# A ring of 24 weight slots, not 20, with rows gathered per expert from the residual stream

## The reference

```
def ec_moe(h, router_w, w_gu, w_down):
    cap = EC_CAPACITY_FACTOR * n // N_EXPERTS          # 32 rows for each expert
    aff = jax.nn.softmax(einsum('bnd,de->bne', h, router_w), axis=-1)
    gates, idx = lax.top_k(jnp.swapaxes(aff, 1, 2), cap)
    xs = jax.vmap(lambda hb, ib: hb[ib])(h, idx)
    ...
        gu = jnp.einsum('bcd,df->bcf', xe, wgu)        # 1024 x 4096 for each expert
        ga, up = jnp.split(gu, 2, axis=-1)
        return jnp.einsum('bcf,fd->bcd', jax.nn.silu(ga) * up, wd)   # 2048 x 1024
    ...  # times the gates, added back to the rows they came from

x = x + ec_moe(rmsnorm_2(x, norm_ffn_g), router_w, expert_w_gu, expert_w_down)
return rmsnorm_2(x, final_norm_g)
```

## Time and profile before

| | |
|---|---|
| median of 3 runs | 1543.46 us (1542.45 to 1544.28) |
| span of the profiled execution | 1539.7 us, from its first to its last instruction; no other time of that execution is given |
| PE, DVE, ACT, POOL busy | 77%, 29%, 25%, 6% of the span |
| moved by DMA | 504.89 MB, of it 493.98 MB on SP's queue |

### The profile page before, as it was taken

One profiled execution on the slowest core, in us unless ns is written; L12 is line 12 of the kernel. 1 busy time (PEld: TensorE's weight loads), 2 busy tenths in 40 slices (PEclk: granted clock), 3 DMA queues, 4 the chain that ended last, 5 costly groups with the idle time before them and its releaser, 6 DMA issues.

```text
span 1539.7 us, 19403 instructions
## 1 busy us (share of the span) xinstructions
PE 1192.7 (77%) x8282; PEld 697.3 (45%) x8282; DVE 443.8 (29%) x867; ACT 381.3 (25%) x847; POOL 87.8 (6%) x95
## 2 busy tenths in 40 slices
PE   7999999999997997986666676666666666666765
PEld 6898989999976775330221211211211212212112
DVE  4565776545678764110000000000000000000002
ACT  4655556444565653110000000000000000000002
POOL 0000010000134420000000000000000000000001
PEclk9999999999999998997877867868767768778666
DMA  8335455454653478999999999999999999999996
GB/s 316 138 137 219 166 189 222 174 195 165 209 191 110 137 273 324 414 421 421 422 421 422 421 422 421 421 421 421 421 422 421 421 422 421 421 421 421 421 421 275
DMA packets 72645, 504.89 MB, mean 328 GB/s; under 512 B 8944, under 2 KB 9584, under 8 KB 12400
## 3 DMA queue, kind: packets, MB, share of 16 engines
q1 hardware_dynamic: 68544, 493.98, 79.3%
q10 hardware_dynamic: 4016, 9.69, 1.8%
HBM read 502.58 MB, written 1.05 MB: 327 GB/s over the span
## 4 chain that ended last, share of the span: by engine, by line
DMA 51%; PE 35%; DVE 5%; ACT 3%; issue 3%; POOL 1%; SPq 1%; ACTq 0%; DVEq 0%; POOLq 0%
DMA RING<-in_wgu_dram 48%; PE PB L99 33%; DMA RING<-in_wdn_dram 2%; PE PB L102 2%; SPq L156 1%; DVE SPL L108 1%; DMA PIOTA<-in_piota_dram 1%; ACT SPH L105 1%; POOL SPL L108 1%; DVE SG L108 1%; ACT SG L105 1%; DVE CO L116 0%; POOL SM L136 0%; ACT HHT L105 0%; DVE AQK L108 0%
## 5 line engine op out<-in xcount | busy, mean ns | idle before, releaser
L99 PE MATMUL PB<-RING,XS 128*32 128x512 f32 x2048 | 374.5, 823 | 201.1 <-DMA RING<-in_wgu_dram 200.3
L99 PEld LDWEIGHTS PB<-RING,XS 128*32 128x32 f32 x2048 | 48.2, 124 | 492.4 <-DMA RING<-in_wgu_dram 471.8
L99 PE MATMUL PB<-RING,HHT 128*32 128x256 f32 x2048 | 167.8, 476 | 71.3 <-DMA RING<-in_wdn_dram 58.9
L108 DVE TENSOR_TENSOR SPL<-RAW,SPH 128x512 fp32r<-128x512 f32 x306 | 202.7, 722 | 38.5 <-ACT SPH L105 36.3
L99 PE MATMUL PB<-XTH,SPL 128*128 128x256 f32 x704 | 202.0, 287 | 0.0
L99 PE MATMUL PB<-XTH,SPH 128*128 128x256 f32 x704 | 199.5, 283 | 0.0
L99 PE MATMUL PB<-XTL,SPH 128*128 128x256 f32 x704 | 199.4, 283 | 0.0
L105 ACT ACTIVATE SPH<-RAW 128x512 fp32r<-128x512 f32 x340 | 186.4, 621 | 4.3 <-issue 1.8
L108 DVE TENSOR_TENSOR SG<-SG,PB 128x512 f32<-128x512 f32 x16 | 11.0, 688 | 575.2 <-ACT SG L105 575.1
L105 ACT ACTIVATE SG<-PB 128x512 f32<-128x512 f32 x16 | 9.6, 597 | 573.4 <-PE PB L99 573.4
L99 PEld LDWEIGHTS PB<-RING,HHT 128*32 128x32 f32 x2048 | 75.0, 132 | 149.9 <-DMA RING<-in_wdn_dram 86.0
(11 more groups left out here) (294 smaller groups left out, 1262.6 us busy)
## 6 DMA issues: line engine op xcount, KB each, us to landing
RING<-in_wgu_dram SPq DMA_DIRECT2D x256, 1024.0 KB, 27.1
RING<-in_wdn_dram SPq DMA_DIRECT2D x128, 1024.0 KB, 27.2
RAW<-in_wst_dram SPq DMA_DIRECT2D x85, 1024.0 KB, 4.8
X<-in_x_dram SPq DMA_DIRECT2D x2, 512.0 KB, 6.7
MEM<-in_mem_dram ACTq DMA_DIRECT2D x1, 1024.0 KB, 7.2
AG<-in_ag_dram ACTq DMA_DIRECT2D x1, 1024.0 KB, 8.9
out_dram<-YG SPq DMA_DIRECT2D x4, 256.0 KB, 2.5
G<-in_mix_pre_g_dram ACTq DMA_DIRECT2D x1, 512.0 KB, 5.4
```

What stands on the lines that cost most here:

```text
L99: return pe.do(lambda e: e.matmul(out_, lhsT, rhs, start=start, stop=stop), after)
L108: return on.do(lambda e: e.tensor_tensor(out_, a, b, op), after)
```

## The change

The ring gets 24 slots of 8 KB (of a partition), from 31 KB up without a hole. Bytes come from these places: the scratch that the program reserves in SBUF for dynamic DMAs is 1 KB, not the default; NX is gone; SEL, XS and the router's tables lie in bytes of the constants and of the turned X below 31 KB; CQ and CPT change places. XS holds the rows of two experts, 32 columns each.

`gather(e)` multiplies X itself with SEL, which carries the row's norm factor in place of the one: `choose` multiplies by `r_tile` (DVE) or uses minus the factor as scale and the factor as bias (ACT). The gain RG is put on when the result leaves PSUM. It runs between the chunks of `k` = 1 and `k` = 2 of the expert before. The load of the gain to G[0] and `normed` are gone; `squares` writes to PSUM.

The ring's first two chunks are issued in the FFN of the first block (group 2 of 5), into the slots 22 and 23, which nothing else uses, without a wait. Five take the waits of `early`; the rest have a new order and new waits.

```diff
-    early = {15: st["read", 3], 10: st["tr", 3], 11: st["values", 3], 12: st["pv", 3], 16: scan_end, 17: scan_end}
-    order = [*early, 19]
...
+    pairs = [2 * (v % NSPLIT) + j for v in range(NU - 4, NU) for j in range(2)]
+    order = [22, 23, 18, 13, 14, 15, 19, 12, 9, 10, 8, 16, 17, *pairs[:4], 11, 20, 21, *pairs[4:]]
...
         if g == 2:
             gw_split = gate_weights()
+            ring_load()
+            ring_load()
...
-    for after in early.values():
+    for after in (st["read", 3], st["tr", 3], st["values", 3], st["pv", 3], scan_end):
         ring_load(after)
...
+            a.append(act(PB[i][:, :], X[:, t, 512 * i:512 * i + 512], ACT.Square, ready[i], *held[i], scale=1.0 / 32, accum_out=q[i]))
...
-    def normed(t, c, r, ready):
-
-        return stt(NX[:, t, c], X[:, t, c], r[0], G[0][:, c], ALU.mult, ALU.mult, r[1], g_ffn2, ready)
...
-    ring_free = {8: [ca["values", 1]], 9: n1, 13: [ca_read], 14: [ca_read], 18: [ca["values", 1]],
-                 19: raw_free[max(v for v in range(NU) if v % NRAW == 1)]}
+    ring_free = {11: [ca["scores", 1]], 12: n1_mem, 16: [ca_read], 17: [ca_read], 20: [scan_end, ca["values", 1]],
+                 21: [ca["values", 1]]}
+    for i in range(NRAW):
+        ring_free[8 + i] = raw_free[max(v for v in range(NU) if v % NRAW == i)]
...
+    r_tile = [r0[0], r1[0]]
+    minus = [small(), small()]
+    minus_ok = [ts(minus[t], r[0], -1.0, None, ALU.mult, None, r[1], on=pool) for t, r in enumerate((r0, r1))]
...
-                a = ts(dst, place_of, PIOTA[:, t:t + 1], None, ALU.is_equal, None, w, *split_done)
+                a = ts(dst, place_of, PIOTA[:, t:t + 1], r_tile[t], ALU.is_equal, ALU.mult, w)
...
-                a = act(dst, dst, ACT.Relu, a, scale=-1.0, bias=1.0)
+                a = act(dst, dst, ACT.Relu, a, minus_ok[t], scale=minus[t], bias=r_tile[t])
...
+    def gather(e):
+
+        for k in range(KD):
+            for t in range(2):
+                w = mm(PB[3][:, 32 * k:32 * k + 32], X[:, t, k * P:(k + 1) * P], SEL[:, t, 32 * e:32 * e + 32],
+                       t == 0, t == 1, *held[3])
+        a = tt(XS[e % 2][:, :, :], PB[3][:, 0:T].rearrange("p (k c) -> p k c", k=KD),
+               RG[:, :].unsqueeze(2).to_broadcast([P, KD, 32]), ALU.mult, w, xs_read.get(e - 2))
...
-        for i in range(max(k - 1, 0), k + (k == KD - 1)):
-            gathered, a = gather(i, slice(32, 512), 6 + i % 2)
-            others.append(a)
     cols_ok = row_columns()
+    gather(1)
     for e in range(16):
...
             for k in range(1, KD):
+                if k == 2 and e < 15:
+                    gather(e + 1)
                 w = expert_in(e, k)
...
-    nc = _bacc.Bacc("TRN2", target_bir_lowering=False, num_devices=1)
+    nc = _bacc.Bacc("TRN2", target_bir_lowering=False, num_devices=1, dynamic_dma_scratch_size=1024)
```

More of the change, by code:

```diff
@@ L266, in build @@
[L266 to L282, removed]
+    RWG = place("RWG", [P, KD, 32], F32, low(8.5))
+    LP = [place(f"LP{i}", [P, P], F32, low(9.5 + i / 2)) for i in range(2)]
@@ new lines, in build @@
+    AFF = place("AFF", [P, 2, 16], F32, low(10.5))
+    COLS = place("COLS", [P, 2, 16], F32, low(10.625))
+    IDXU = place("IDXU", [16, 32], U32, low(10.75))
+    IDXF = place("IDXF", [16, 32], F32, low(10.875))
+    GATE = place("GATE", [16, 32], F32, low(11))
+    REP = place("REP", [16, 2, 4, 32], F32, low(11.125))
+    SEL = place("SEL", [P, 2, 512], F32, at(23))
+    BD = place("BD", [16, 4, 16, 8], F32R, at(27))
+    AFT = [place(f"AFT{i}", [16, T], F32, at(29 + i)) for i in range(2)]
+    XS = [place(f"XS{i}", [P, KD, 32], F32, at(15 + i)) for i in range(2)]
@@ new lines, in build @@
+    SG = place("SG", [P, 512], F32, at(17))
+    HHT = place("HHT", [P, 4, P], F32, at(19))
+    YH = [place(f"YH{i}", [P, T], F32R, at(21 + i)) for i in range(2)]
+    YL = [place(f"YL{i}", [P, T], F32R, at(27 + i)) for i in range(2)]
+    IOTA = place("IOTA", [P, T], F32, at(29))
+    SQ = place("SQ", [P, T], F32, at(30))
+    GT = [place(f"GT{i}", [P, T], F32R, low(8.5 + i)) for i in range(2)]
+    RING = [place(f"RING{i}", [P, UNIT], F32, at(31 + 8 * i)) for i in range(24)]
+    YG = place("YG", [P, 2, D], F32, at(31 + 8 * 22))
@@ L810, in gate_weights, with ring_load @@
         return l
+    NR = len(RING)
+    pairs = [2 * (v % NSPLIT) + j for v in range(NU - 4, NU) for j in range(2)]
+    order = [22, 23, 18, 13, 14, 15, 19, 12, 9, 10, 8, 16, 17, *pairs[:4], 11, 20, 21, *pairs[4:]]
+    s_r = [sem(f"s_r{i}") for i in range(NR)]
+    ring = {"n": 0}
+    chunk_in, chunk_slot = [], []
+    def ring_load(*after):
+        n = ring["n"]
+        if n >= 16 * 24:
+            return
+        ring["n"] += 1
+        e, i = divmod(n, 24)
+        src = io["wgu"][8 * e + i // 2, :, UNIT * (i % 2):UNIT * (i % 2) + UNIT] if i < 16 else io["wdn"][8 * e + i - 16]
+        i = order[n % NR]
+        chunk_slot.append(i)
+        chunk_in.append(load(sp, RING[i][:, :], src, s_r[i], 16 * (n // NR + 1), *after))
     f = 0
@@ L1438, in build @@
     u += 4
-    n0 = [normed(0, slice(512 * i, 512 * i + 512), r0, xs[0][i]) for i in range(2)]
     lg0 = router_logits(0, lp0)
@@ L1507, in build, with gather_first @@
         choose(*at_)
[L1508 removed]
+    rep = [copy(REP[:, j, :, :], src[:, :].unsqueeze(1).to_broadcast([16, 4, 32]), xf, m, on=pool)
            for j, src in enumerate((IDXF, GATE))]
[L1512 removed]
+    iota_in = load(act_l, IOTA[:, :], io["iota"], sem("s_iota"), 16, ix)
+    xs_ok, xs_read = {}, {}
     st = {"n": 0}
[L1515 to L1517 removed]
+    def gather_first(k):
+        b = 4 + k % 2
         for t in range(2):
[L1519 to L1527 removed]
+            w = mm(PB[b][:, 0:32], X[:, t, k * P:(k + 1) * P], SEL[:, t, 0:32], t == 0, t == 1, *sel, *xs[t], *held[b])
+        xs_ok[0, k] = act(XS[0][:, k, :], PB[b][:, 0:32], ACT.Copy, w, scale=RG[:, k:k + 1])
+        held[b] = [xs_ok[0, k]]
+    def gather(e):
[5 more added lines that the diff above has]
+               RG[:, :].unsqueeze(2).to_broadcast([P, KD, 32]), ALU.mult, w, xs_read.get(e - 2))
+        held[3] = [a]
+        for k in range(KD):
+            xs_ok[e, k] = a
     def expert_in(e, k):
@@ L1568, in expert_out @@
         y, gate = PB[b][:, 0:T], COLS[:, 1, e:e + 1]
-        h = act(YH[m % 2][:, :], y, ACT.Copy, w, st.get(("y", m % 2)), cols_ok, gathered, scale=gate)
+        h = act(YH[m % 2][:, :], y, ACT.Copy, w, st.get(("y", m % 2)), cols_ok, scale=gate)
         l = stt(YL[m % 2][:, :], y, gate, YH[m % 2][:, :].bitcast(F32), ALU.mult, ALU.subtract, h, st.get(("y", m % 2)))
@@ L1621, in build @@
     s_out = sem("s_out")
[L1622 to L1623 removed]
+    gu_done = w
+    g_fin = load(act_l, GF[:, :], row("final_norm_g_2", D), sem("s_gf"), 16, gu_done)
     ms = [small(4), small(4)]
```

124 lines of the change are left out of this document (41 added, 83 removed).

## The result

The changed kernel takes 1532.24 us (median of 4 runs, 1527.53 to 1534.42); the kernel before, in the same session, 1542.95 (1540.43 to 1544.28). The ratio is 0.9929 [0.9911, 0.9947]: 10.7 us less, where 10.2 less were forecast. The profiled execution is the slowest of the four, 1534.42 with a span of 1532.7, and that span is 7.0 under the one of before, not 10.2.

The account below looks back on a forecast made before the run. The prediction took the full DMA stream of ring chunks as the bound: start, slope, tail. The ring's 10.0 us plus 0.2 from PE's start, gathers and tail at nothing, took 1543.46 to 1533.2 us; range 1530.0 to 1537.0.

Parts of the forecast that it names:

- The ring's 10.0 us: Weight stream: four more chunks loaded before PE frees its first slot, at 2.506 us each, save 10.0 us.
- Chunk 24 at 612.3: Ring fill: the last of 24 chunks lands at 612.3 us, just when the first refill is issued.
- The other end of the range: Ring fill at 346 GB/s: chunk 24 lands at 619.4 us and 3.4 of the 10.0 us are lost.
- PE 0.2 earlier: PE's start on the first chunk, after router and selection: 0.2 us earlier through DVE passes removed.
- Same shape, same engine: Selection compares and squares before PE's start: reason for costing both at 0; compares could cost 0 to 0.6 us.
- Gathers hidden: Expert loop: per-expert gathers of 5.0 to 8.2 us lie beside the stream and add 0; uncovered, 123 us.
- Tail 11.2: After the last landing: stays 11.2 us, already at the lower clock, so can't get slower; could gain 2 us.
- The sum: Whole kernel: 10.0 + 0.2 = 10.2 us off, span 1529.5, timed median 1533.2 us.
- Late fill: Rival, ring fill: chunk 24 lands behind the first refill, 1536.7 or 1537.7 us; 3.1 to 8 off, chance 0.18.
- PE the bound: Rival, expert loop: PE at the lower clock needs 61.6 us an expert, over 60.1, giving 1556 us; chance 0.04.
- Hidden anyway: Rival, weight stream: its start is set elsewhere, so the added slots give nothing, 1543 us; chance 0.05.
- The shallower queue: Rival, DMA queue with smaller scratch: one chunk at a time, 5.4 not 2.5 us, 1000 us more; chance 0.01.

Follow-up runs that it names:

- Experiment 1: The changed kernel with 20 ring slots instead of 24, everything else of the change kept: 1542.12 us, 0.9994 of the kernel before.
- experiment 4: The changed kernel with chunk 11 also waiting for the cross attention's last value product, so the fill is late: 1543.17 us, 1.0002 of the kernel before.
- experiment 3: The changed kernel with the two free slots loaded after the mixer's loads, not in the first block's FFN: 1532.59 us, 0.9935 of the kernel before.
- 5: The changed kernel with each expert's gather on PE made twice: 1534.02 us, 0.9948 of the kernel before.
- 10: The changed kernel with expert 15's second-quarter down products issued before the first combine: 1530.68 us, 0.9924 of the kernel before.
- 12: The changed kernel run again, unchanged, in a later session: 1531.69 us, 0.9934 of the kernel before.
- experiment 6: The changed kernel with each expert's gather on PE made four times: 1557.52 us, 1.0084 of the kernel before.
- experiment 8: The changed kernel with 13 unread PE products before the first chunk and expert 15's down products of quarters 1 and 2 each one combine earlier: 1532.92 us.

## Why the prediction was right, point by point

**The ring's 10.0 us.** Right. Experiment 1 takes them back, experiment 4 takes them back with the slots in place, and the place of the first two chunks is free, as the prediction costed it; experiment 3 shows that it wasn't even needed. The condition it named, all 24 loaded in time, is the one that decides: the last of them lands half a microsecond behind the first refill's issue in the changed kernel and 15.5 behind it in experiment 4. The size is 9.2 by the profiles, from PE's first chunk to the last landing.

**Chunk 24 at 612.3.** 613.7 came. Chunk 11's split on POOL ends 0.5 later (570.97 + 4.09 = 575.06), since matmuls at 491 to 496 us ran at a lower granted clock in this execution (0.50 for 0.65; PB<-AG,UP takes 3.68 for 3.19 us); most of the rest is one gap in the queue at 601, where chunk 19 lands 3.15 behind chunk 18. By the prediction's own numbers chunk 21 had a margin of 604.9 - 597.3 = 7.6 us and not "9 us or more"; in the run chunks 19 to 24 land 11.2 us or more behind their issues. The other end of the range, 346 GB/s through the fill, did not occur: 384, then 421.

**PE 0.2 earlier.** Wrong in sign. PE starts at 611.16, 0.5 of it that shift, and the chain from the end of the output product to the first chunk is 13.35 us long for 13.19. The second factor of the selections is not free. The view of SEL's instructions shows it, before (count, ns min/median/max):

```profile
L105 ACT ACTIVATE SEL<-SEL x4: 308/309/310, 605.6 to 607.5; 128x128 f32<-128x128 f32 x4
L112 DVE TENSOR_SCALAR SEL<-PB,PIOTA x4: 343/346/351, 607.7 to 608.6; 128x128 f32<-128x128 f32 x4
```

and after:

```profile
L105 ACT ACTIVATE SEL<-SEL,SM x4: 492/492/493, 606.1 to 608.4; 128x128 f32<-128x128 f32 x4
L113 DVE TENSOR_SCALAR SEL<-PB,PIOTA,SM x4: 400/400/409, 608.1 to 609.1; 128x128 f32<-128x128 f32 x4
```

"Same shape, same engine" was the step that failed: scale and bias that differ by row, in place of two constants, cost 183 ns on ACT, and a second factor by row with its multiplication 54 ns on DVE, at this shape. The DVE four end the chain, 1.36 us for the 1.24 of before, and the first XS copy with its scale, which the prediction had no term for, takes 0.29 for 0.20: together 0.2. The passes removed from DVE gave less, since where the last of them stood DVE now waits for PE:

```profile
603.05 0.42 DVE L143 MAX8 GATE<-PB 16x8 f32<-16x256 f32 x1 [0.48 <-PE PB L102]
```

MAX8 starts 603.05 - 597.81 = 5.24 us behind the output product's end, for 602.61 - 597.31 = 5.30 before. That is the 0.06 that the passes gave here; the chain is 13.24 or 13.25 us long in the profiles of experiments 1, 3, 4, 5, 10 and 12, where they gave about 0.1 more. The squares were costed right at nothing: 0.60 us into PSUM for 0.63 into SBUF. The Trainium skill (ScalarE: Activation LUTs, 🔬 ACT is a hardware spline evaluator) states that ScalarE writes PSUM faster than SBUF; the trace agrees, by 0.03 us.

**Gathers hidden.** Right. They take 4.5 us at expert 0 and 58.2 / 12 = 4.85 on average, just under the 5.0 to 8.2 and over the 3.4 that the prediction estimated from weight loads, and PE waits 15.9 us an expert, more than the 10 to 14 forecast, since its other products are recorded shorter. Twice the gathers stay hidden. The reason given, a queue of eleven chunks, was too small a cover for the stream, where the ring itself covers, and too large a one for experts 0 and 1, where experiment 6 ran the queue dry.

**Tail 11.2.** Right on average, 1.5 too short for the profiled execution, which has 12.7. Nine profiles have the changed kernel's router and its order in the tail; their tails are 9.8 to 12.7 us long, 11.4 in the mean, and the kernel before has 11.2. In the seven of them at a granted clock of 0.71 in the 16 us ahead of the last landing it is 10.9 to 12.7, in the two at 0.82 and 0.90 it is 10.2 and 9.8. So "it can't get slower by the clock" failed: it looked at the 11.2 us behind the last landing and forgot what PE owes when it lands. PE in the tail of the changed kernel:

```profile
1504.25 3.64 PE L99 MATMUL PB<-RING,HHT 128*32 128x256 f32 x32 [0.78 <-ACT HHT L105]
...
1510.21 3.45 PE L99 MATMUL PB<-RING,HHT 128*32 128x256 f32 x32
...
1515.52 1.93 PE L99 MATMUL PB<-RING,HHT 128*32 128x256 f32 x32
1519.83 0.36 PE L99 MATMUL PB<-YL,GT 128*128 128x256 f32 x1 [2.38 <-DVE YL L116]
...
1520.67 3.34 PE L99 MATMUL PB<-RING,HHT 128*32 128x256 f32 x32
```

A quarter at the lower of the two levels (3.64 for 32 passes, which take 1.93 at the higher) takes 1510.21 - 1504.25 = 5.96 with its combine, two loads only 2 x 2.49 = 4.98. The third combine then waits 2.38 for YL, where the others wait 1.2, since ACT's YH stands behind squares, as in experiment 8. So PE falls behind the landings, and its last product ends 4.0 behind the last one, for 2.2 before. How much of this is the clock and how much the order on ACT, no run shows apart.

**The sum.** In the profiled execution the terms are 621.85 - 621.20 = 0.65 later at chunk 26 where 0.2 earlier was forecast, 358 x (2.5087 - 2.5064) = 0.8 of pace, and 1.5 of tail: 3.2 of the 10.2, which leaves the 7.0 that its span shows. The medians of several runs differ by 10.7, since this execution is the slowest of four; the same kernel's other profile has a span of 1526.2. Single runs of the changed kernel in that session lie between 1527.53 and 1534.42, and in the session of experiment 12 the medians differ by 10.2. So 10 us is what the change gives; that the median stands within half a microsecond of the ring's 10.0 and the start's 0.2 is luck, since the first measured 9.2 and the second had the wrong sign.

**The rivals.** Late fill: not here, and experiment 4 shows that it would have cost all. PE the bound: not in the stream. Hidden anyway: fallen by experiment 1. The shallower queue: fallen, 27.2 us between issue and landing for 27.1, share 1.01 at 1 KB; this agrees with the rule of the Trainium skill (DMA: Bandwidth & Descriptors, SWDGE vs HWDGE vs iDMA) that the prediction weighed, by which SP's DMAs never touch the rings in that scratch.

## What to carry to other kernels

A deeper ring in front of a stream that is bound by its transfers is worth its added slots times the pace, once, and only if all slots are loaded about when the first one comes free: look for the fill's latest free slot first. Work on an engine that waits for the stream is free in the middle of it, and dear at the start, where that engine is a ring behind. A tail is to be read from what the engine still owes when the last transfer lands, at the clock it has then, and from more than one execution: here it moved by 3 us without a change to its code.

## What the runs showed of the hardware that was not expected

- Scale and bias by row, in place of constants, make ACT's 128x128 pass 0.49 us for 0.31; a scale by row alone makes the XS copy (128x32) 0.29 for 0.20. A second factor by row makes DVE's 128x128 compare 0.40 for 0.346.
- PE started its first chunk between 605.66 and 611.16 us in two executions of the same kernel, and the span followed, 1526.2 and 1532.7.
- 13 products in PE's waits held the granted clock at 0.97 from 602 to 606 us (PE busy 2.41 of 4.00), but not for the first two chunks (0.50 from 606 to 609.7; 3.33 us for 3.64).
- SP issued three chunks at 575.1 to 576.0 and they landed 5.4, 7.5 and 9.5 us later: into an empty queue a chunk takes 5.4 us here and 4.7 to 5.4 as the first refill of the runs whose fill is in time, and each chunk behind it about 2.5 more.
